# Layer 0's first phase and layer 1's stick-breaking heads in another order

## Chip, core and metric

The kernel runs on one core of one Trainium2 chip. The time is the device time of one execution in microseconds. Three runs of the kernel before gave 1487.02, 1489.60 and 1493.04 us.

## What is computed

A two-layer causal decoder trunk for one sequence of 512 tokens, 1024 wide, in float32. Both touched stages start from the adaLN modulation and end in a projection:

```python
c_act = jax.nn.silu(c)
mod = c_act @ ada_w[layer] + ada_b[layer]
sh_m, sc_m, g_m, sh_f, sc_f, g_f = [t[:, None, :] for t in jnp.split(mod, 6, axis=-1)]
hm = x * (1.0 + sc_m) + sh_m
...
z = jnp.einsum('bqhd,bkhd->bhqk', q_blk, k) * scale
causal = s_pos[None, :] < t_pos[:, None]
log_1m = jnp.where(causal, jax.nn.log_sigmoid(-z), 0.0)
suffix = lax.cumsum(log_1m, axis=3, reverse=True)
excl = jnp.pad(suffix[..., 1:], ((0, 0), (0, 0), (0, 0), (0, 1)))
att = jnp.where(causal, jnp.exp(jax.nn.log_sigmoid(z) + excl), 0.0)
return jnp.einsum('bhqk,bkhd->bqhd', att, v)
...
y = jnp.concatenate([oc, od], axis=-1) @ w_out
```

The first four lines open both touched mixers; the next are one block of 128 queries of the eight stick-breaking heads of layer 1, whose output `oc` is joined with `od` of the dilated attention (three groups of four heads, merged by their softmax denominators). Layer 0 projects `hm` for gated linear attention and mLSTM.

## The kernel before

Every large product is made of three matmuls: the float32 operands are split into a high part (`w_hi`, `h_hi`) and a rest (`w_lo`, `h_lo`), and hi x lo, hi x hi and lo x hi are added in PSUM. Weights come as a stream of slots of 128x1024. SP loads slot s into one of four `raw` buffers, ACT makes `w_hi` (`to_hi`, L690), POOL makes `w_lo` (L670), and TensorE uses both from a ring of four. ACT's order is written by hand: `hi_until(n)` makes all splits up to slot n, and `ahead(name)` those for a stage and three more. TensorE waits for a slot in `slot_waits`, and reports it used with `slot_done`.

**First phase.** The shift and scale of layer 0 are needed in quarters: quarter p covers chunks 2p and 2p+1 of the 1024 features. For each quarter DVE multiplies eight blocks of `ada_first` by the columns of `c_act` and adds them up in `ada_acc` (`first_block`, 128x512 each, L1631 and L1634). TensorE then sums over the partitions, four matmuls against a column of ones (`first_cols`, L1175), DVE adds the bias (`first_mod`, L1641, L1643), ACT scales the input chunk into `tmp` (`x_scaled`, L719) and makes `h_hi` (L704), DVE makes `h_lo` (L1570). TensorE then does the 18 matmuls of chunk k, 12 for `va` and 6 for `qa` (`first_va`, `first_qa`). All four quarters run one after another; the narrow projection follows.

**Layer 1.** After the panels of q, k and v of the stick-breaking heads, each head h goes through: `sb_z` (TensorE, scores into 1280 columns of PSUM), Abs, Exp, Ln (ACT, `sb_first`), softplus and two masks (DVE, `softplus`, L2025, L2027), `sb_tri` (TensorE adds the suffix sums to the same PSUM columns), Exp (ACT, `sb_second`), two masks (DVE, `att_mask`), `sb_av` (TensorE). Between them stand the fillers, the list `FILL`: six panels of 48 matmuls (two slots each) for q and k of the dilated heads, and the two groups `vd0` (four slots) and `vd1` (two slots) of their values. With filler i stands either tri (i even) or av and the next z (i odd), so that the eight fillers lie in heads 0 to 3; heads 4 to 7 follow without. Here z of one head can be issued ahead, since odd heads above 4 use other PSUM columns (`sb_col`). Each pair of heads fills one chunk of the input of the output projection: DVE copies it to `tmp` and ACT and DVE split it (`sb_chunk`). Then come 16 score steps of the dilated heads (TensorE, L1497), each read by DVE (L2077, with maxima L2082), the turned maxima, and the transposes and products of the dilated heads (`turn_round`, `pv_round`), and `out1`.

## Time and profile before

| | |
|---|---|
| median of three runs | 1489.6 us |
| the profiled execution | 1487.6 us |
| its span, first to last instruction | 1485.8 us |
| mean granted TensorE clock | 0.959 |
| TensorE matmul, busy | 1366.9 us (92%) |
| TensorE weight load | 1123.3 us (76%) |
| DVE | 622.7 us (42%) |
| ACT | 449.3 us (30%) |
| POOL | 506.8 us (34%) |

The span is 1.8 us shorter than the time of that execution. Times in the trace are counted from the span's start. A busy TensorE is not one at its peak, since the ends of matmuls are modelled; consecutive matmuls overlap in the rows.

### The profile page before, as it was taken

Reading aid. Unit: us, or ns where it says so; the run is one execution under the profiler, and the core shown is the slowest. Engines: PE = TensorE matmul, PEld = TensorE weight load, DVE = VectorE, ACT = ScalarE, POOL = GpSimd, SP = SyncE. Lnnn points to the kernel's source line nnn. Section 1 sums busy time; section 2 is a strip of 40 time slices with the busy share of each in tenths; the row PEclk is TensorE's granted clock in tenths of the full one; section 3 lists DMA queues with packets and bytes.
Section 4 is the critical chain, followed back from the end, with each engine's and each line's share of the span. In section 5 each row is a group of like instructions: output and inputs, shape, how many; then the busy total and the mean of one; then the engine's idle time right before and its main releaser. Section 6 shows DMA issues by size and latency. Waiting matters only on the chain.

```text
span 1485.8 us, 17068 instructions
## 1 busy us (share of the span) xinstructions
PE 1366.9 (92%) x6510; PEld 1123.3 (76%) x6510; DVE 622.7 (42%) x830; ACT 449.3 (30%) x603; POOL 506.8 (34%) x209
## 2 busy tenths in 40 slices
PE   3799998798999999999899999887889999999995
PEld 3678776588888888888788778656779888887884
DVE  5569751858643433400882232226486111010007
ACT  2343233314233223212323323333233323322121
POOL 2334331024345344444243333100125444444440
PEclk9899998799999999999999999997999999999998
DMA  9493632042556546643235322001113232234311
GB/s 335 134 97 102 212 117 82 22 176 72 181 175 209 197 152 232 182 126 100 104 116 180 109 85 72 29 1 57 36 50 100 99 99 99 92 79 154 99 57 56
DMA packets 93456, 173.79 MB, mean 117 GB/s; under 512 B 15655, under 2 KB 61879, under 8 KB 93276
## 3 DMA queue, kind: packets, MB, share of 16 engines
q1 hardware_dynamic: 90264, 169.63, 36.8%
q10 hardware_dynamic: 3140, 3.43, 0.9%
q8 instruction: 38, 0.62, 0.2%
q14 instruction: 14, 0.11, 0.0%
HBM read 170.87 MB, written 4.52 MB: 118 GB/s over the span
## 4 chain that ended last, share of the span: by engine, by line
PE 64%; issue 22%; DVE 6%; POOL 6%; ACT 2%; POOLq 0%; DVEq 0%; ACTq 0%
PE ps L1018 12%; PE ps L1020 12%; PE ps L1019 12%; PE ps L1050 6%; PE ps L1051 6%; PE ps L1052 6%; POOL w_lo L670 6%; PE ps L1462 1%; PE ps L1143 1%; PE ps L1145 1%; PE ps L1144 1%; PE ps L1434 1%; PE ps L1445 1%; PE ps L1448 1%; DVE rec L2101 1%
## 5 line engine op out<-in xcount | busy, mean ns | idle before, releaser
L670 POOL TENSOR_TENSOR w_lo<-raw,w_hi 128x1024 fp32r<-128x1024 f32 x205 | 506.6, 2474 | 943.8 <-ACT w_hi L690 943.4
L1018 PE MATMUL ps<-h_lo,w_hi 128*128 128x512 f32 (+2 forms) x1064 | 401.6, 377 | 13.6 <-DVE tmp L1867 6.2
L1019 PE MATMUL ps<-h_hi,w_hi 128*128 128x512 f32 (+2 forms) x1064 | 398.0, 374 | 0.0
L1020 PE MATMUL ps<-h_hi,w_lo 128*128 128x512 f32 (+2 forms) x1064 | 397.4, 374 | 0.0
L690 ACT ACTIVATE w_hi<-raw 128x1024 fp32r<-128x1024 f32 x205 | 216.0, 1056 | 487.8 <-PE ps L1052 189.0
L1018 PEld LDWEIGHTS ps<-h_lo,w_hi 128*128 128x128 f32 (+1 forms) x1064 | 204.1, 192 | 54.4 <-DVE tmp L1867 7.5
L1020 PEld LDWEIGHTS ps<-h_hi,w_lo 128*128 128x128 f32 (+1 forms) x1064 | 203.9, 192 | 35.1
L1019 PEld LDWEIGHTS ps<-h_hi,w_hi 128*128 128x128 f32 (+1 forms) x1064 | 203.9, 192 | 34.0
L1951 DVE TENSOR_TENSOR tmp<-tmp,ps 128x512 f32<-128x512 f32 x44 | 30.1, 688 | 264.2 <-PE ps L1020 264.2
L1050 PE MATMUL ps<-w_hi,hid_lo 128*128 128x512 f32 x352 | 137.9, 392 | 1.8 <-issue 0.9
L1052 PE MATMUL ps<-w_lo,hid_hi 128*128 128x512 f32 x352 | 137.5, 390 | 0.0
L1051 PE MATMUL ps<-w_hi,hid_hi 128*128 128x512 f32 x352 | 137.4, 390 | 0.0
L1901 DVE TENSOR_TENSOR ps<-ps,gate_ffn 128x1024 f32<-128x1024 f32 x8 | 9.8, 1229 | 184.5 <-PE ps L1052 184.5
L1050 PEld LDWEIGHTS ps<-w_hi,hid_lo 128*128 128x128 f32 x352 | 66.5, 189 | 16.1 <-issue 1.3
L1586 DVE SCALAR_TENSOR_TENSOR ada_acc<-ada_raw,c_act,ada_acc 128x1024 f32<-128x1024 f32 x35 | 63.4, 1813 | 35.3 <-DMA ada_raw<-astream 34.3
L1051 PEld LDWEIGHTS ps<-w_hi,hid_hi 128*128 128x128 f32 x352 | 66.5, 189 | 13.7
L1052 PEld LDWEIGHTS ps<-w_lo,hid_hi 128*128 128x128 f32 x352 | 66.4, 189 | 13.8
L1970 DVE SCALAR_TENSOR_TENSOR ada_acc<-ada_raw,c_act,ada_acc 128x1024 f32<-128x1024 f32 x35 | 54.8, 1565 | 46.5 <-DMA ada_raw<-astream 46.1
L1143 PE MATMUL ps<-w_hi,h_lo 128*128 128x512 f32 (+1 forms) x192 | 74.1, 386 | 0.0
L1144 PE MATMUL ps<-w_hi,h_hi 128*128 128x512 f32 (+1 forms) x192 | 72.8, 379 | 0.0
L1145 PE MATMUL ps<-w_lo,h_hi 128*128 128x512 f32 (+1 forms) x192 | 72.7, 379 | 0.0
L908 ACT ACTIVATE hid_hi<-tmp 128x512 f32 (+1 forms) x44 | 27.5, 631 | 88.5 <-DVE tmp L1951 88.5
(228 smaller groups left out, 1491.5 us busy)
## 6 DMA issues: line engine op xcount, KB each, us to landing
raw<-wstream SPq DMA_DIRECT2D x205, 512.0 KB, 4.1
ada_raw<-astream SPq DMA_DIRECT2D x80, 512.0 KB, 4.6
ada_first<-astream SPq DMA_DIRECT2D x12, 512.0 KB, 10.0
ln_rows<-row_scratch SPq DMA_DIRECT2D x3, 1024.0 KB, 6.8
skew_scratch<-f_scratch ACTq DMA_DIRECT2D x1, 2304.0 KB
ada_first<-astream SPq DMA_DIRECT2D x8, 256.0 KB, 4.6
xa<-xT SPq DMA_DIRECT2D x4, 512.0 KB, 9.4
out<-xa SPq DMA_DIRECT2D x4, 512.0 KB, 3.5
```

Of the source, the lines that this page charges most:

```text
L670: nc.gpsimd.tensor_tensor(w_lo[:, slot, :], raw[:, slot % RAW, :], w_hi[:, slot, :].bitcast(F32), ALU.subtract).then_inc(sem("w_lo_ready"), 1)
L690: nc.scalar.activation(w_hi[:, slot, :], raw[:, slot, :], ACT.Copy).then_inc(sem("w_hi_ready"), 1)
L1018: pe.matmul(o, w_h, x_l, start=start, stop=False)
L1019: pe.matmul(o, w_h, x_h, start=False, stop=False)
L1020: return pe.matmul(o, w_l, x_h, start=False, stop=stop)
L1050: pe.matmul(o, x_lo, w_h, start=k == 0, stop=False)
L1051: pe.matmul(o, x_hi, w_h, start=False, stop=False)
L1052: m = pe.matmul(o, x_hi, w_l, start=False, stop=k == nk - 1)
L1143: pe.matmul(o, h_lo[:, k, tokens], w_hi[:, s % RING, w], start=start, stop=False)
L1144: pe.matmul(o, h_hi[:, k, tokens], w_hi[:, s % RING, w], start=False, stop=False)
L1145: m = pe.matmul(o, h_hi[:, k, tokens], w_lo[:, s % RING, w], start=False, stop=stop)
L1586: V.scalar_tensor_tensor(ada_acc[:], src, c_act[:, k:k + 1], ada_acc[:], ALU.mult, ALU.add).then_inc(sem("ada_step"), 1)
```

## The change

In the first phase the first slot of weights is loaded behind the first pair of `ada_first` and split before anything else on ACT. DVE adds up only six of eight blocks per quarter (`ON_DVE`); the products of blocks 6 and 7 are made by TensorE, added in PSUM to the column sums, so that `first_cols` has twelve matmuls in place of four. The column sums of quarter p+1 are issued between the two chunks of quarter p, and DVE's steps for the next quarter stand between the two `h_lo` of this one.

In layer 1 the fillers alternate q and k panels, with `vd1` before `vd0`, and one filler stands with each of the eight heads. All heads use the same PSUM columns and one bank for av; z(h+1) waits for the Exp of head h (`att_exp`). `vd0` has two slots with head 7, the third before av(7) and the fourth behind score step 3. The score steps use banks 4 to 7. The finished chunks are staged (`staged`) in `ada_acc` and `tmp`, and split only after the heads: the hi on ACT behind the copies of `vd0`, the lo on DVE behind `nm`.

```diff
@@ -91,14 +91,20 @@
+ON_DVE = 6
...
+FILL = ("qd0", "kd0", "qd1", "kd1", "qd2", "kd2", "vd1", "vd0")
+MIXED = [n for n in STAGES if n not in FILL]
+MIXED[MIXED.index("out10"):MIXED.index("out10")] = FILL
 def slot_table():
...
-    for name in STAGES:
+    for name in MIXED:
@@ -407,15 +410,12 @@
-    AV_BANK = (7, 7, 7, 3)
-    def sb_col(h):
-        return 0 if h > 4 and h % 2 else 4 * S
-    FILL = [f"qd{p}" for p in range(3)] + [f"kd{p}" for p in range(3)] + ["vd0", "vd1"]
+    AV_BANK = 7
+    SB_COL = 4 * S
+    def staged(n):
+        return ada_acc[:, n * S:(n + 1) * S] if n < 2 else tmp[:, n % 2, :]
@@ -448,7 +448,7 @@
     def score_bank(s):
...
-        return (0, 1, 2, 4)[2 * (part % 2) + h % 2]
+        return 4 + 2 * (part % 2) + h % 2
     def part_tiles(part):
@@ -571,10 +571,11 @@
-        for k in range(0, KC, 2):
+        load_pair(0, 0, 2)
+        load(0)
+        for k in range(2, KC, 2):
...
-        load(0)
@@ -719,12 +720,13 @@
+        hi_until(1)
         for p in range(4):
             for n in (2 * p, 2 * p + 1):
...
-                if p == 0:
-                    hi_until(n + 1)
+                if n == 0:
+                    hi_until(2)
...
         def x_chunk(n):
@@ -955,32 +957,31 @@
         def sb_second(h):
...
-            nc.scalar.activation(sb_a[h % 2][:], psf[:, sb_col(h):sb_col(h) + SC], ACT.Exp).then_inc(sem("att_exp"), 1)
+            nc.scalar.activation(sb_a[h % 2][:], psf[:, SB_COL:SB_COL + SC], ACT.Exp).then_inc(sem("att_exp"), 1)
...
-        for i, part in enumerate(FILL):
-            if part[0] == "v":
+        for h, part in enumerate(FILL):
+            if part == "vd0":
+                hi_until(SLOTS[part][0] + 2 + RING)
+            elif part[0] == "v":
...
-            if i == 1:
+            if h == 1:
...
-            if i % 2 == 0:
-                sb_second(i // 2)
-            else:
-                sb_first(i // 2 + 1)
-        hi_of_chunk(H_BASE["cat1"], 0)
-        for h in range(4, 8):
+            sb_second(h)
...
-            sb_second(h)
-            if h % 2 == 0:
-                hi_of_chunk(H_BASE["cat1"] + h // 2 - 1, h // 2 - 1)
-        hi_of_chunk(H_BASE["cat1"] + 3, 3)
+        hi_until(SLOTS["vd0"][0] + 4 + 2)
+        v_blocks("vd0", v_dst["vd0"])
+        for n in range(4):
+            e = H_BASE["cat1"] + n
+            act.wait_ge(sem("h_tmp_ready"), e + 1)
+            nc.scalar.activation(h_hi[:, n, :], staged(n), ACT.Copy).then_inc(sem("h_hi_ready"), 1)
         def dil_exp(h, kind):
@@ -1123,11 +1124,12 @@
-        def group(name, kk_n, width, beside=None):
+        def group(name, kk_n, width, beside=None, only=None):
...
-            wait_pair(pe, name)
-            for i in range(count):
+            if only is None or 0 in only:
+                wait_pair(pe, name)
+            for i in range(count) if only is None else only:
@@ -1168,11 +1170,17 @@
         def first_cols(p):
-            pe.wait_ge(sem("first_step"), KC * (p + 1))
+            pe.wait_ge(sem("c_ready"), 1)
+            pe.wait_ge(sem("first_step"), ON_DVE * (p + 1))
+            if p == 0:
+                pe.wait_ge(sem("in_ada0_6"), 32)
             for blk in range(2):
...
-                    m = pe.matmul(ps[:, 6 + p % 2, 2 * blk + c:2 * blk + c + 1], ada_acc[:, a:a + P], ones[:], start=True, stop=True)
+                    o = ps[:, 6 + p % 2, 2 * blk + c:2 * blk + c + 1]
+                    pe.matmul(o, ada_acc[:, a:a + P], ones[:], start=True, stop=False)
+                    for k in range(ON_DVE, KC):
+                        m = pe.matmul(o, ada_first[:, p, k, blk, tile_of(c)], c_act[:, k:k + 1], start=False, stop=k == KC - 1)
...
         def first_va(k):
@@ -1200,16 +1208,18 @@
+        first_cols(0)
         for p in range(4):
-            first_cols(p)
             for k in (2 * p, 2 * p + 1):
...
-                    if k in (0, 2, 4, 6):
+                    if k % 2 == 0 and part is first_va:
...
-                    if k in (0, 4):
+                    if k in (0, 4) and part is first_qa:
...
+                if k % 2 == 0 and p < 3:
+                    first_cols(p + 1)
@@ -1423,13 +1433,11 @@
         def sb_z(h):
...
-            base = sb_col(h)
+            base = SB_COL
...
-            elif h <= 4:
+            else:
...
-            elif h >= 6:
-                pe.wait_ge(sem("att_exp"), h - 1)
@@ -1454,50 +1462,51 @@
-            if h == 2:
-                pe.wait_ge(sem("staged"), 1)
-            if h == 4:
-                pe.wait_ge(sem("h_tmp_ready"), H_BASE["cat1"] + 2)
+            if h in (2, 4, 6):
+                pe.wait_ge(sem("h_tmp_ready"), H_BASE["cat1"] + h // 2)
...
-                m = pe.matmul(ps[r:r + 64, AV_BANK[c], j * P:S], vc[:, j, h * 64:h * 64 + 64], sb_a[h % 2][:, OFS[j]:OFS[j] + WID[j]],
+                m = pe.matmul(ps[r:r + 64, AV_BANK, j * P:S], vc[:, j, h * 64:h * 64 + 64], sb_a[h % 2][:, OFS[j]:OFS[j] + WID[j]],
...
-        for i, part in enumerate(FILL):
-            if part[0] == "v":
-                group(part, 2 if part == "vd0" else 4, S if part == "vd0" else 256)
+        for h, part in enumerate(FILL):
+            if part == "vd0":
+                group(part, 2, S, only=(0, 1))
+            elif part == "vd1":
+                group(part, 4, 256)
...
-            if i % 2 == 0:
-                sb_tri(i // 2)
-            elif i < 7:
-                sb_av(i // 2)
-                sb_z(i // 2 + 1)
-        sb_z(4)
-        wait_free(pe, "vd1")
-        wait_free(pe, "vd1+")
-        for h in range(4, 8):
+            sb_tri(h)
+            if h:
+                sb_av(h - 1)
...
-            sb_av(h - 1)
-            sb_tri(h)
+        group("vd0", 2, S, only=(2,))
...
-        pe.wait_ge(sem("att_exp"), 8)
-        for s in range(16):
+        def scores(s):
...
+            if score_bank(s) == AV_BANK:
+                pe.wait_ge(sem("h_tmp_ready"), H_BASE["cat1"] + 4)
...
+        for s in range(4):
+            scores(s)
+        group("vd0", 2, S, only=(3,))
+        for s in range(4, 16):
+            scores(s)
@@ -1538,7 +1547,8 @@
-        pe.wait_ge(sem("h_tmp_ready"), H_BASE["cat1"] + 4)
+        wait_free(pe, "vd0")
+        wait_free(pe, "vd0+")
@@ -1618,19 +1628,18 @@
-        def first_block(p):
+        def first_block(p, ks):
...
-            if p >= 2:
-                dve.wait_ge(sem("first_cols"), p - 1)
-            for k in range(KC):
-                step = KC * p + k
+            for k in ks:
...
+                    if p >= 2:
+                        dve.wait_ge(sem("first_cols"), p - 1)
...
-                    dve.wait_ge(sem("first_step"), step)
+                    dve.wait_ge(sem("first_step"), ON_DVE * p + k)
@@ -1642,11 +1651,21 @@
-        for p in range(4):
-            first_block(p)
+        first_block(0, range(ON_DVE))
+        first_mod(0)
+        lo_of_chunk(H_BASE["in"], 0)
+        lo_of_chunk(H_BASE["in"] + 1, 1)
+        first_block(1, range(ON_DVE))
+        for p in range(1, 4):
...
-            for n in (2 * p, 2 * p + 1):
-                lo_of_chunk(H_BASE["in"] + n, n)
+            if p < 3:
+                first_block(p + 1, range(0, 2))
+            lo_of_chunk(H_BASE["in"] + 2 * p, 2 * p)
+            if p < 3:
+                first_block(p + 1, range(2, 4))
+            lo_of_chunk(H_BASE["in"] + 2 * p + 1, 2 * p + 1)
+            if p < 3:
+                first_block(p + 1, range(4, ON_DVE))
...
         def v_blocks(name):
@@ -2033,38 +2052,28 @@
-        def sb_chunk(n):
-            e = H_BASE["cat1"] + n
+        def stage(n):
...
-            tmp_free(e)
-            src = ada_acc[:, 0:S] if n == 0 else ps[:, AV_BANK[n], :]
-            V.tensor_copy(tmp[:, e % 2, :], src).then_inc(sem("h_tmp_ready"), 1)
-            lo_of_chunk(e, n)
+            V.tensor_copy(staged(n), ps[:, AV_BANK, :]).then_inc(sem("h_tmp_ready"), 1)
+        def lo_of_staged(n):
+            dve.wait_ge(sem("h_hi_ready"), H_BASE["cat1"] + n + 1)
+            V.tensor_tensor(h_lo[:, n, :], staged(n), h_hi[:, n, :].bitcast(F32), ALU.subtract).then_inc(sem("h_ready"), 1)
...
-        for i, part in enumerate(FILL):
-            if part[0] == "v":
+        for h, part in enumerate(FILL):
+            if part == "vd1":
...
-            else:
+            elif part != "vd0":
...
-            if i % 2 == 0:
-                att_mask(i // 2)
-            else:
-                if i == 3:
-                    dve.wait_ge(sem("av_done"), 2)
-                    V.tensor_copy(ada_acc[:, 0:S], ps[:, AV_BANK[0], :]).then_inc(sem("staged"), 1)
-                softplus(i // 2 + 1)
-        dve.wait_ge(sem("staged"), 1)
-        sb_chunk(0)
-        for h in range(4, 8):
+            att_mask(h)
+            if h in (2, 4, 6):
+                stage(h // 2 - 1)
...
-            att_mask(h)
-            if h % 2 == 0:
-                sb_chunk(h // 2 - 1)
-        sb_chunk(3)
+        stage(3)
@@ -2081,6 +2090,7 @@
+        v_blocks("vd0")
@@ -2088,6 +2098,8 @@
+        for n in range(4):
+            lo_of_staged(n)
         def dil_out(h):
```

ACT at the start of the program, before:

```order
L711 ACTIVATE c_act<-vec 128x8
L719 ACTIVATE tmp<-xa,mod,scl 128x512
L704 ACTIVATE h_hi<-tmp 128x512
L690 ACTIVATE w_hi<-raw 128x1024
L719 ACTIVATE tmp<-xa,mod,scl 128x512
L704 ACTIVATE h_hi<-tmp 128x512
L690 ACTIVATE w_hi<-raw 128x1024 x2
L719 ACTIVATE tmp<-xa,mod,scl 128x512
```

and now:

```order
L712 ACTIVATE c_act<-vec 128x8
L691 ACTIVATE w_hi<-raw 128x1024
L720 ACTIVATE tmp<-xa,mod,scl 128x512
L705 ACTIVATE h_hi<-tmp 128x512
L691 ACTIVATE w_hi<-raw 128x1024
L720 ACTIVATE tmp<-xa,mod,scl 128x512
L705 ACTIVATE h_hi<-tmp 128x512
L691 ACTIVATE w_hi<-raw 128x1024
```

The first split of a weight has moved ahead of the first scaled chunk, the second stands between the first two chunks.

DVE in the first phase, from the first accumulation of quarter 1 on, before:

```order
L1631 TENSOR_SCALAR ada_acc<-ada_first,c_act 128x512
L1634 SCALAR_TENSOR_TENSOR ada_acc<-ada_first,c_act,ada_acc 128x512 x7
L1641 TENSOR_TENSOR mod<-ps,vec 128x2x2
L1643 TENSOR_SCALAR scl<-mod 128x2
L1570 TENSOR_TENSOR h_lo<-tmp,h_hi 128x512 x2
L1631 TENSOR_SCALAR ada_acc<-ada_first,c_act 128x512
L1634 SCALAR_TENSOR_TENSOR ada_acc<-ada_first,c_act,ada_acc 128x512 x7
```

and now:

```order
L1640 TENSOR_SCALAR ada_acc<-ada_first,c_act 128x512
L1643 SCALAR_TENSOR_TENSOR ada_acc<-ada_first,c_act,ada_acc 128x512 x5
L1650 TENSOR_TENSOR mod<-ps,vec 128x2x2
L1652 TENSOR_SCALAR scl<-mod 128x2
L1640 TENSOR_SCALAR ada_acc<-ada_first,c_act 128x512
L1643 SCALAR_TENSOR_TENSOR ada_acc<-ada_first,c_act,ada_acc 128x512
L1580 TENSOR_TENSOR h_lo<-tmp,h_hi 128x512
L1643 SCALAR_TENSOR_TENSOR ada_acc<-ada_first,c_act,ada_acc 128x512 x2
L1580 TENSOR_TENSOR h_lo<-tmp,h_hi 128x512
L1643 SCALAR_TENSOR_TENSOR ada_acc<-ada_first,c_act,ada_acc 128x512 x2
L1650 TENSOR_TENSOR mod<-ps,vec 128x2x2
```

A quarter has six accumulations in place of eight; those of quarter 2 now stand around the two `h_lo` of quarter 1.

TensorE in layer 1, from the last matmul of tri(5) to the first of tri(6), before (L1434 is z, L1462 is av, L1445 is tri):

```order
L1445 MATMUL ps<-sb_sp_113,cst 128x128
L1434 MATMUL ps<-qc,kc 128x512
L1434 MATMUL ps<-qc,kc 128x384
L1434 MATMUL ps<-qc,kc 128x256
L1434 MATMUL ps<-qc,kc 128x128
L1462 MATMUL ps<-sb_a_111,vc 64x512
L1462 MATMUL ps<-sb_a_111,vc 64x384
L1462 MATMUL ps<-sb_a_111,vc 64x256
L1462 MATMUL ps<-sb_a_111,vc 64x128
L1445 MATMUL ps<-sb_sp_112,cst 128x512
```

and now, from the last matmul of a tri to the first of the panel behind the next z (L1453 is tri, L1468 is av, L1442 is z, L1019 to L1021 are a panel's):

```order
L1453 MATMUL ps<-sb_sp_112,cst 128x128
L1468 MATMUL ps<-sb_a_111,vc 64x512
L1468 MATMUL ps<-sb_a_111,vc 64x384
L1468 MATMUL ps<-sb_a_111,vc 64x256
L1468 MATMUL ps<-sb_a_111,vc 64x128
L1442 MATMUL ps<-qc,kc 128x512
L1442 MATMUL ps<-qc,kc 128x384
L1442 MATMUL ps<-qc,kc 128x256
L1442 MATMUL ps<-qc,kc 128x128
L1019 MATMUL ps<-h_lo,w_hi 128x512
L1020 MATMUL ps<-h_hi,w_hi 128x512
L1021 MATMUL ps<-h_hi,w_lo 128x512
```

Where tri(6) followed av(5) directly, a filler of 48 matmuls now stands behind z.

## Rows read from the trace of the kernel before

**Rows 1.** The page, part 1: busy time of each engine, share of the span, instructions.
```profile
PE 1366.9 (92%) x6510; PEld 1123.3 (76%) x6510; DVE 622.7 (42%) x830; ACT 449.3 (30%) x603; POOL 506.8 (34%) x209
```

**Rows 2.** Windows, first phase: stretch, length, busy us per engine (count), clock, DMA.
```profile
0.00:22.90 22.90, 1.89 (x9) 1.83 (x9) 10.80 (x15) 6.16 (x8) 5.30 (x6) 1.00 0.94 317
...
66.70:76.50 9.80, 9.80 (x36) 7.97 (x37) 1.42 (x3) 3.52 (x5) 4.73 (x2) 0.83 0.71 55
```

**Rows 3.** Timeline, DVE, first phase: start, us, engine, line, operation, tiles, count.
```profile
9.60 3.18 DVE L1634 SCALAR_TENSOR_TENSOR ada_acc<-ada_first,c_act,ada_acc 128x512 f32<-128x512 f32 x4 [0.87 <-DMA ada_first<-astream]
...
14.74 0.16 DVE L1641 TENSOR_TENSOR mod<-ps,vec 128x4 f32<-128x4 f32 x1 [1.96 <-PE ps L1175]
...
16.64 0.69 DVE L1570 TENSOR_TENSOR h_lo<-tmp,h_hi 128x512 fp32r<-128x512 f32 x1 [1.54 <-ACT h_hi L704]
...
23.06 7.47 DVE L1634 SCALAR_TENSOR_TENSOR ada_acc<-ada_first,c_act,ada_acc 128x512 f32<-128x512 f32 x7
...
39.43 9.63 DVE L1634 SCALAR_TENSOR_TENSOR ada_acc<-ada_first,c_act,ada_acc 128x512 f32<-128x512 f32 x7
```

**Rows 4.** Timeline, TensorE, first phase.
```profile
12.83 1.87 PE L1175 MATMUL ps<-ones,ada_acc 128*128 128x1 f32 x8 [12.83 <-DVE ada_acc L1634]
...
22.88 0.77 PE L1185 MATMUL ps<-w_hi,h_lo 128*128 128x512 f32 x1 [8.18 <-POOL w_lo L670]
...
49.11 1.49 PE L1175 MATMUL ps<-ones,ada_acc 128*128 128x1 f32 x8 [2.97 <-DVE ada_acc L1634]
53.29 0.80 PE L1185 MATMUL ps<-w_hi,h_lo 128*128 128x512 f32 x1 [2.69 <-DVE h_lo L1570]
...
63.04 0.95 PE L1175 MATMUL ps<-ones,ada_acc 128*128 128x1 f32 x8
```

**Rows 5.** Timeline, ACT, first phase: the first half of a weight split.
```profile
16.52 1.04 ACT L690 ACTIVATE w_hi<-raw 128x1024 fp32r<-128x1024 f32 x1
```

**Rows 6.** Windows, layer 1, head 0 to the start of out1.
```profile
813.50:947.10 133.60, 133.60 (x608) 109.35 (x608) 32.35 (x30) 43.86 (x44) 43.57 (x18) 0.98 0.28 87
947.10:998.90 51.80, 42.14 (x154) 24.34 (x153) 15.87 (x27) 21.80 (x19) 0.00 (x0) 0.93 0.00 0
998.90:1020.30 21.40, 13.59 (x121) 12.72 (x120) 20.37 (x27) 0.63 (x1) 0.00 (x0) 0.81 0.16 41
1020.30:1057.60 37.30, 27.08 (x201) 25.19 (x201) 23.57 (x20) 17.98 (x42) 0.00 (x0) 0.82 0.08 33
```

**Rows 7.** Timeline, head 1 of layer 1, all engines, in order of time.
```profile
846.44 1.24 ACT L950 ACTIVATE sb_a<-ps 128x1280 f32<-128x1280 f32 x1 [6.77 <-PE ps L1434]
...
851.32 4.95 POOL L670 TENSOR_TENSOR w_lo<-raw,w_hi 128x1024 fp32r<-128x1024 f32 x2 [11.37 <-ACT w_hi L690]
851.85 4.70 DVE L2027 TENSOR_TENSOR sb_sp<-sb_sp,cst 128x256 f32<-128x256 f32 x2
...
857.39 1.02 PE L1445 MATMUL ps<-sb_sp,cst 128*128 128x512 f32 x2
...
861.92 1.24 ACT L958 ACTIVATE sb_a<-ps 128x1280 f32<-128x1280 f32 x1 [6.46 <-PE ps L1445]
...
872.73 2.37 PE L1462 MATMUL ps<-sb_a,vc 128*64 128x512 f32 x8
```

**Rows 8.** Timeline, heads 4 to 6 of layer 1, DVE and TensorE.
```profile
954.99 0.76 DVE L2027 TENSOR_TENSOR sb_sp<-sb_sp,cst 128x256 f32<-128x256 f32 x2
955.81 1.13 PE L1445 MATMUL ps<-sb_sp,cst 128*128 128x512 f32 x2 [2.34 <-DVE sb_sp L2027]
...
961.74 2.42 PE L1434 MATMUL ps<-qc,kc 64*128 64x512 f32 x8 [1.33 <-ACT sb_a L958]
```

**Rows 9.** Waits, 813 to 1058 us: waited for, us in total, times, longest.
```profile
PE ps L1462 <- DVE sb_a L2033: 4.6, 2, 2.5
```

**Rows 10.** Timeline, DVE, score steps and first turn copy.
```profile
1006.40 2.21 DVE L2077 TENSOR_TENSOR lg_loc<-ps,bt 128x512 f32<-128x512 f32 x4
...
1028.82 0.69 DVE L2109 COPY pt<-ps 128x512 f32<-128x512 f32 x1 [3.86 <-PE ps L1522]
```

More of the change, by code:

```diff
@@ L333, in last @@
         return first + n - 1
-    V_FREE = {"va": 0, "vb": 1, "vc": 2, "vd0": 3, "vd1": 4}
+    V_FREE = {"va": 0, "vb": 1, "vc": 2, "vd1": 3, "vd0": 4}
     def group(name, free0, free1):
@@ L357, in build_program @@
             if layer == 1:
-                for i, (name, panels) in enumerate((("qc", 2), ("kc", 2), ("qd", 3), ("kd", 3))):
-                    base = (0, 2, 4, 7)[i]
-                    for p in range(panels):
-                        e = base + p
-                        use(f"{name}{p}", [("qk1_act", e + 1), ("qk1_dve", e + 1)], last(f"{name}{p}"))
-                    if name == "kc":
+                for e, name in enumerate(("qc0", "qc1", "kc0", "kc1") + FILL[:6]):
+                    use(name, [("qk1_act", e + 1), ("qk1_dve", e + 1)], last(name))
+                    if name == "kc1":
                         vgroup("vc")
+                vgroup("vd1")
                 vgroup("vd0")
-                vgroup("vd1")
         else:
@@ L944, in sb_first @@
         def sb_first(h):
-            z = psf[:, sb_col(h):sb_col(h) + SC]
+            z = psf[:, SB_COL:SB_COL + SC]
             a = sb_a[h % 2]
@@ L1438, in sb_tri @@
         def sb_tri(h):
-            base = sb_col(h)
+            base = SB_COL
             sp_ = sb_sp[h % 2]
@@ L2024, in softplus @@
             sp_ = sb_sp[h % 2]
-            link(V.scalar_tensor_tensor(sp_[:], psf[:, sb_col(h):sb_col(h) + SC], 0.0, sb_a[h % 2][:], ALU.max, ALU.add))
+            link(V.scalar_tensor_tensor(sp_[:], psf[:, SB_COL:SB_COL + SC], 0.0, sb_a[h % 2][:], ALU.max, ALU.add))
             for t in diag_tiles(sp_):
```

## The prediction

> **What bounds the kernel now.** The page says that TensorE is busy 1366.9 of 1485.8 us, a share of 92% [rows 1]. The other engines only matter where TensorE waits for them, so I read its waits stage by stage. The windows give two stages that the diff touches. The first phase, to the start of the narrow projection at 76.5 us: no real matmul runs before 22.9 us, and from 66.7 to 76.5 us the granted clock is 0.83 of full [rows 2]. The stick-breaking stage of layer 1: from 813.5 to 947.1 us TensorE has no idle time (133.60 of 133.60), from 947.1 to 998.9 it is busy 42.14 of 51.80, from 998.9 to 1020.3 busy 13.59 of 21.40 while DVE is busy 20.37 [rows 6]. So in the last window DVE sets the pace; in the one before it the heads 4 to 7 do, one after another, with nothing to fill their waits.
>
> The timelines say what those waits are. First phase: the column sums of a quarter wait for DVE's last accumulation (49.11, idle 2.97), and the first chunk behind them waits 2.69 us for the chain mod, scale, x_scaled, hi, lo (53.29) [rows 4]; that matmul takes 0.80 us, at the slow level of the clock (1.2 GHz), and the next six are as slow. Layer 1: tri(4) waits 2.34 us, z(6) 1.33 and z(7) the same again [rows 8], av(6) and av(7) 4.6 us together [rows 9]: 9.6 us in all.
>
> **Layer 1, part by part.** One filler now goes with each of the eight heads, where eight fillers went with heads 0 to 3. The fillers' work is the same, save that the last slot of vd0 moves behind four score steps. Its price is one quarter of vd0, 24 matmuls. A panel has 48: tri(1) and the panel behind it take 872.73 - 857.39 = 15.3 us [rows 7], tri(4) alone 961.74 - 1.33 - 955.81 = 4.6 [rows 8] with some 0.2 of overlap, so the panel is 10.9 us and a matmul 0.227. The slot is 24 x 0.227 = 5.5 us.
>
> - Full-clock work in 947.1 to 998.9: tri 4 x 4.5, av 5 x 2.3, z 4 x 2.4 [rows 7, 8] = 39.1 us. The window lasts 51.8: 9.6 idle and 3.0 slow clock are over it.
> - With a filler behind every z the same work is issued in 133.6 + 39.1 us less the moved slot, 5.5, plus one new wait: z(1) follows tri(0) with no av between them and waits for the Exp, 1.3 us. From head 1 on, av(h-1), 2.3 us, stands where this 1.33 us wait was, and hides it. av(7) ends at 813.5 + 133.6 + 39.1 - 5.5 + 1.3 = 982.0, so 16.9 us earlier.
> - Is the softplus in time for each tri? Abs, Exp and Ln start at 846.44 behind z(1); DVE's masks end at 851.85 + 4.70 = 856.55; tri(1) starts at 857.39 [rows 7]. That is the situation in which every head now is: 0.8 us to spare. If the cover were gone, each head would wait.
> - ACT carries per head 4 x 1.25 for the head [rows 7] and 2 x 1.05 for splits [rows 5], with a panel copy under 8 of some 20 us; its Exp is queued behind two weight splits, which have long been done when tri ends [rows 7]. POOL does two splits of 2.5 us per head. The four hi and four lo of the staged chunks go behind the heads: ACT has nothing to do there until nm is ready, and DVE waits 3.86 us before its first turn copy [rows 10], against 4 x 0.69 = 2.8 for the lo. The stage copies (0.69) stand while ACT works on z. Hidden, all of it. vd0's two DVE copies, 1.4 us, lie in the transposes that DVE waits for. If that cover goes, 1.4 us come back.
> - The bias loads, the row order of weights and SP's queue keep their order relative to the slots; no transfer is added.
> - Score steps: DVE needs stage, memset and steps 0 to 3 with their maxima, some 0.7 + 0.5 + 4.8 = 6.0 us behind av(7). TensorE does four steps (2.8; sixteen took 13.59 at clock 0.81 [rows 6], 0.7 each at the full one), the slot (5.5) and step 4 (0.7) = 9.0. DVE so waits 3.0 us, then does the rest, 1006.40 to 1020.3 = 13.9 [rows 6, 10]: 22.9 against 21.4 now (where a hi and a lo stood in the way). **1.5 us are given back.** Layer 1: -16.9 + 1.5 = **-15.4 us**. Bounds: -19 if DVE were never held up and the stretch at the end kept the full clock, -7 if each head waited 1 us.
>
> **First phase, part by part.**
> - Raw 0 is loaded and split first. Its POOL split (some 2.5 us, half of 4.95 [rows 7]) now stands beside the first accumulations. DVE steps cost 0.80 us (3.18 for four) [rows 3]. Two drop out, -1.6; the 0.5 MB that now go ahead and POOL's presence take about as much. I take 0; bounds -1.6 and +2.5, one POOL split.
> - Column sums have 24 records in place of 8. They took 1.87 us for the first quarter, 1.49 at the half clock, 0.95 at the full one [rows 4]: three times as much less the fixed part is 5.3 at the slow level and 2.8 at the fast one. So +3.4 for the first, then 3 x 1.9.
> - The first chunk no longer waits for w_lo. It started at 22.88 after a wait for POOL [rows 4], though h_lo was done at 17.33 [rows 3]. Now mod is at 12.8 + 5.3 = 18.2, and h_lo, as much behind it as before (17.33 - 14.74 = 2.6), at 20.8. The chunk starts **2 us** earlier.
> - Column sums of quarter p+1 stand between the two chunks of quarter p. The 2.69 waits (three) disappear under them. But DVE has to be in time. Quarter 1: hi(1) is done at 18.2 + 1.9 + a split of 1.04 [rows 5] + 1.4 = 22.5, lo(1) comes behind POOL's split of slot 1 and ends at 24.3. Six steps take 4.3 us of their own and lose 2.2 to one split (7.47 for seven steps where 5.3 is their own time [rows 3]): 30.8. TensorE does the first chunk, 14 matmuls at 0.43 and 4 at 0.23, by 28.0 and waits 2.8; sums to 33.6. Quarter 2: DVE's mod, two steps, lo, two steps, lo take to 38.4, the last two steps 1.5 and 4.4 lost to two splits (9.63 for seven [rows 3]), some 0.5 of it over before: 43.8, TensorE 33.6 + 8.2 = 41.8, it waits 2.0; sums to 46.6. Quarter 3: DVE 51.4 + 1.5 + 2.2 = 55.1, TensorE 54.8; sums to 57.9, three more chunks of 4.1.
> - The last chunk ends at 70.2 against 76.5 in this reckoning at the full clock, -6.3. But a wait of 2 to 3 us followed by column sums is what stood before the slow matmuls at 53.29 and 66.7 (clock 0.83, [rows 2, 4]): 7 or 8 matmuls at 0.43 in place of 0.23 are 1.5 us each time. Twice, with half absorbed where DVE is late anyway: +1.8. First phase: **-4.5 us**. Bounds: -11, if DVE is in time and the clock stays up; +2, if all waits stay and both slow stretches too.
>
> At one place a rule can be weighed. The two masks of 128x256 took 4.70 us beside 4.95 us of POOL splits and 0.76 alone [rows 7, 8], a loss of 3.94. The Trainium skill, page "SBUF — State Buffer", section "Who interferes with whom", says that DVE and GpSimd share one port pair as an exclusive lock and the one that comes second is held up entirely. By that rule taken to its end the masks lose the whole 4.95, 1.0 us more, which is 0.2 beyond the slack; the sum would be 8 x 0.2 = 1.6 us worse. The sum goes by the measured row.
>
> **The sum.** -15.4 - 4.5 = -19.9. The profiled execution took 1487.6 us outside (span 1485.8 and 1.8 around it): 1487.6 - 19.9 = 1467.7, so **1468 us**. That execution stood 2.0 us below the median of the runs, 1489.6.
>
> **The rivals.** About 0.5% (7.4 us) is what a measurement can tell; the line for faster is 1482 us.
> 1. The first phase gives nothing: longer column sums and DVE's lateness eat the earlier start. For it: both chains I computed leave 2 to 3 us waits. Then 1487.6 - 15.4 = 1472.
> 2. The masks come late at every head, by 1.5 us: two splits fall on each softplus, and the slack is 0.8 us. 8 x 1.5 = 12, so 1480. Against it: just this overlap is there now, in time [rows 7].
> 3. More than the forecast: DVE in time in the first phase, clock full in both places, 1487.6 - 28 = 1460.
> 4. **Slower.** z(h+1) uses the same PSUM columns as head h and now waits at each head for its Exp, so all heads form one loop: z 2.4, Abs to Ln 3.9, DVE 6.3, tri 4.5, Exp 1.3 = 18.4 us, against 20.2 us of TensorE work per head (panel 10.9, tri, av, z). ACT's Exp is queued behind weight splits: where a weight lands late, the Exp is late. The loop decides from 20.2 us on; the gain is gone at 23 us, and it is slower by 0.5% from 24.1. At 26 us: 7 x 5.8 = 41, 1508. Against it: TensorE was never idle in 813.5 to 947.1 [rows 6], so no weight was late.
> 5. The diff does not fill the heads (order of slots and fillers out of step): no change, 1488. The order of instructions shows panels behind z(5) to z(7), so next to nothing.
>
> **How the numbers follow.** Forecast 0.62 (1460 to 1475), rival 1 0.15, rival 2 0.10, rival 3 0.10, rival 4 0.02, rival 5 0.01. The range 1459 to 1478 holds the forecast, rivals 1 and 3 and the edge of rival 2; 0.15 lies outside. Faster: 0.62 + 0.15 + 0.10 and half of rival 2, 0.92. Same: the other half, rival 5 and a little for tails, 0.06. Slower 0.02.
>
> **What would show it.** Right: no idle time on TensorE from tri(1) to av(7) and av(7) near 978 on the new time axis (982 less 4.5); z(1) waiting 1.3; DVE waiting some 3 us before score step 4; the first 128x512 matmul near 21 us and the narrow projection near 72; column sums of 24 records at 2.8 us or more. Wrong: waits before each tri (rival 2), before each z (rival 4), or a narrow projection at 76 or later (rival 1).

## The result, and the profile after

| | median us | lowest to highest | runs |
|---|---|---|---|
| before | 1491.14 | 1487.02 to 1493.04 | 4 |
| changed | 1472.15 | 1469.38 to 1474.12 | 4 |

The ratio is 0.9891, with a 95% interval from 0.987 to 0.9912: 1.1% faster, inside the range of 1459 to 1478, 4 us above the forecast of 1468, and just where rival 1 stood (1472). That ratio, which is not the quotient of the two medians, stands for 16 us; the medians are 19.0 us apart. The profiled execution took 1471.77 us (span 1470.0), against 1487.59 (span 1485.8) before: 15.8 us less, where the sum said 19.9. Of the runs of the kernel before that stand beside experiments 5 to 8 one took 4254.8 us; the ratios leave it out.

**Layer 1.** Windows of the changed kernel from z(1) to the start of out1; the columns are those of [rows 6].

```profile
832.30:982.30 150.00, 149.98 (x669) 114.38 (x669) 55.85 (x47) 54.09 (x50) 36.94 (x15) 1.00 0.19 60
982.30:1006.10 23.80, 16.96 (x145) 16.11 (x144) 19.80 (x27) 3.27 (x6) 0.00 (x0) 0.85 0.14 54
1006.10:1042.30 36.20, 25.94 (x201) 24.05 (x201) 27.15 (x26) 18.01 (x42) 0.00 (x0) 0.83 0.02 10
```

From z(1) to av(7) TensorE is never idle. Its waits from 815 to 985 us, over all lines, are one row:

```profile
PE ps L1442 <- ACT sb_a L960: 1.3, 1, 1.3
```

That is the wait of z(1) for the Exp that the forecast named. The rest is told by these rows of the changed kernel's timelines: POOL and DVE in head 2, TensorE at tri(2), and DVE at the score steps.

```profile
859.74 4.93 POOL L671 TENSOR_TENSOR w_lo<-raw,w_hi 128x1024 fp32r<-128x1024 f32 x2 [15.14 <-ACT w_hi L691]
860.28 4.68 DVE L2046 TENSOR_TENSOR sb_sp<-sb_sp,cst 128x256 f32<-128x256 f32 x2
865.77 1.02 PE L1453 MATMUL ps<-sb_sp,cst 128*128 128x512 f32 x2
...
979.98 2.37 PE L1468 MATMUL ps<-sb_a,vc 128*64 128x512 f32 x8
982.38 0.69 DVE L2058 COPY tmp<-ps 128x512 f32<-128x512 f32 x1 [8.50 <-PE ps L1468]
992.21 2.22 DVE L2086 TENSOR_TENSOR lg_loc<-ps,bt 128x512 f32<-128x512 f32 x4 [3.44 <-PE ps L1500]
1006.14 1.86 PE L1515 MATMUL ps<-cst,cols 128*4 128x128 f32 x8 [5.24 <-DVE cols L2091]
```

The masks end at 864.96, tri(2) starts at 865.77: the 0.8 us of slack, the same in heads 1 to 5; heads 6 and 7 have 1.3 to 1.4. av(7) is done at 982.3, where the forecast said 982.0 before it took off the 4.5 us of the first phase. DVE then waits 3.44 us for score step 4 (forecast 3.0).

**First phase.** Timeline of TensorE in the changed kernel. Column sums are now printed by pairs of rows, x2 on L1181 (ones) and x4 on L1183 (the two products), four pairs per quarter; the first row of each quarter's sums and the first of the chunk behind them:

```profile
14.29 0.56 PE L1181 MATMUL ps<-ones,ada_acc 128*128 128x1 f32 x2 [14.29 <-DVE ada_acc L1643]
...
22.23 0.80 PE L1193 MATMUL ps<-w_hi,h_lo 128*128 128x512 f32 x1 [2.69 <-DVE h_lo L1580]
...
32.09 0.35 PE L1181 MATMUL ps<-ones,ada_acc 128*128 128x1 f32 x2 [3.67 <-DVE ada_acc L1643]
...
36.41 0.77 PE L1193 MATMUL ps<-w_hi,h_lo 128*128 128x512 f32 x1
...
47.00 0.35 PE L1181 MATMUL ps<-ones,ada_acc 128*128 128x1 f32 x2 [0.57 <-DVE ada_acc L1643]
...
59.58 0.28 PE L1181 MATMUL ps<-ones,ada_acc 128*128 128x1 f32 x2
```

And DVE's: the last four accumulations of quarter 0, the first and the last mod (the shift and scale of a quarter, with the bias added), and two of the places where POOL's splits hold it.

```profile
9.23 4.95 DVE L1643 SCALAR_TENSOR_TENSOR ada_acc<-ada_first,c_act,ada_acc 128x512 f32<-128x512 f32 x4 [2.33 <-DMA ada_first<-astream]
19.58 0.16 DVE L1650 TENSOR_TENSOR mod<-ps,vec 128x4 f32<-128x4 f32 x1 [5.39 <-PE ps L1183]
...
25.34 2.61 DVE L1640 TENSOR_SCALAR ada_acc<-ada_first,c_act 128x512 f32<-128x512 f32 x1
...
41.16 5.69 DVE L1643 SCALAR_TENSOR_TENSOR ada_acc<-ada_first,c_act,ada_acc 128x512 f32<-128x512 f32 x2
...
62.35 0.16 DVE L1650 TENSOR_TENSOR mod<-ps,vec 128x4 f32<-128x4 f32 x1 [4.25 <-PE ps L1183]
```

DVE ends quarter 0 at 14.18 though it does two steps fewer; it ended at 12.78 before [rows 3]. The first sums take from 14.29 to 19.5, the first chunk starts at 22.23 (22.88 before [rows 4]), and every later mod comes later than the forecast had it. The narrow projection starts at 76.15, against 76.52 before: in this trace the first phase gives 0.4 us of the 4.5 forecast, which is what rival 1 said.

TensorE's waits up to 76 us say where the gain went, first of the kernel before, then of the changed one (us in total, times, longest):

```profile
PE ps L1175 <- DVE ada_acc L1634: 15.8, 2, 12.8
PE ps L1185 <- POOL w_lo L670: 8.2, 1, 8.2
PE ps L1185 <- DVE h_lo L1570: 8.1, 3, 2.7
```

```profile
PE ps L1181 <- DVE ada_acc L1643: 18.5, 3, 14.3
PE ps L1193 <- DVE h_lo L1580: 2.7, 1, 2.7
```

The waits fell from 32.1 to 21.2 us, 10.9 less. The four sets of column sums took 5.25 us before and take 14.8 now, 9.6 more, and the 144 matmuls of the chunks took 39.2 and take 40.1, 0.9 more. The order did remove waits; the longer sums used them up.

### The profile page after: what moved, and what is told of

Its sections match the earlier page's. It is cut to its first block, busy times and chain, and to the rows that moved or that the text cites. A ratio compares the mean times of both kernels' runs of the same rounds, so it can differ in the third digit from the quotient of the medians.

```text
span 1470.0 us, 17183 instructions
## 1 busy us (share of the span) xinstructions
PE 1371.6 (93%) x6574; PEld 1131.7 (77%) x6574; DVE 636.7 (43%) x821; ACT 449.1 (31%) x603; POOL 513.7 (35%) x209
## 4 chain that ended last, share of the span: by engine, by line
PE 80%; DVE 10%; issue 6%; ACT 1%; POOL 1%; DMA 0%; DVEq 0%; POOLq 0%; ACTq 0%
PE ps L1019 14%; PE ps L1020 14%; PE ps L1021 14%; PE ps L1051 7%; PE ps L1052 7%; PE ps L1053 7%; PE ps L1145 2%; PE ps L1147 2%; PE ps L1146 2%; PE ps L1442 1%; POOL w_lo L671 1%; PE ps L1468 1%; PE ps L1456 1%; PE ps L1453 1%; PE ps L1158 1%
## 5 line engine op out<-in xcount | busy, mean ns | idle before, releaser
L671 POOL TENSOR_TENSOR w_lo<-raw,w_hi 128x1024 fp32r<-128x1024 f32 x205 | 513.5, 2509 | 921.1 <-ACT w_hi L691 920.6
L1019 PE MATMUL ps<-h_lo,w_hi 128*128 128x512 f32 (+2 forms) x1064 | 403.2, 379 | 13.1 <-DVE tmp L1886 6.2
L1021 PE MATMUL ps<-h_hi,w_lo 128*128 128x512 f32 (+2 forms) x1064 | 398.7, 375 | 0.0
L1019 PEld LDWEIGHTS ps<-h_lo,w_hi 128*128 128x128 f32 (+1 forms) x1064 | 204.9, 193 | 53.4 <-DVE tmp L1886 7.5
L1021 PEld LDWEIGHTS ps<-h_hi,w_lo 128*128 128x128 f32 (+1 forms) x1064 | 204.9, 193 | 35.1
L1053 PEld LDWEIGHTS ps<-w_lo,hid_hi 128*128 128x128 f32 x352 | 66.1, 188 | 13.9
```

The costliest lines, as they stand in the source:

```text
L671: nc.gpsimd.tensor_tensor(w_lo[:, slot, :], raw[:, slot % RAW, :], w_hi[:, slot, :].bitcast(F32), ALU.subtract).then_inc(sem("w_lo_ready"), 1)
L1019: pe.matmul(o, w_h, x_l, start=start, stop=False)
L1021: return pe.matmul(o, w_l, x_h, start=False, stop=stop)
L1053: m = pe.matmul(o, x_hi, w_l, start=False, stop=k == nk - 1)
```

## The experiments

Theory A: layer 1 gives what the sum said, and the first phase next to nothing, because (i) the two products of each quarter cost TensorE more than the two steps cost DVE, and (ii) w 0 ahead of the weights of quarter 0 makes DVE late, by its transfer and by POOL's split. Rival B: the first phase did gain its 4.5 us, and another stage lost them. The mark for the first phase is the start of va's first eviction on ACT (74.30 in the changed kernel, 74.67 before). Each median stands beside before's on the same chip: 1487.57 for 1 to 4, 1487.23 for 5 to 8, 1486.94 for the rest.

**1 and 2. Each half of the change alone.** e1 has the first phase of before: `for p in range(4): first_block(p); first_mod(p)`, then the two lo, `first_cols(p)` ahead of both chunks, eight accumulations per quarter, and w 0 (the first slot of weights) at its old place. e2 has before's layer 1.

> The first phase of the kernel before, layer 1 of the changed one. Theory A (layer 1 gives all the gain, the first phase 0.4 us, read at va's first copy: 74.30 in the changed kernel, 74.67 before): about 1472.5 us, ratio to before 0.990, va's first copy at 74.7, av(7) starting at 980.4, the first turn of the first output at 1013. Rival B (the first phase does give its 4.5 us and later stages lose them again): about 1476, and somewhere behind 75 us a stretch that is shorter here than in the changed kernel.

> The first phase of the changed kernel, layer 1 of the one before. Theory A: within 1 us of before, ratio 0.9995, va's first copy at 74.3. Rival B: 4.5 us less than before, ratio 0.997.

e1: 1472.47, ratio 0.9901 (0.988 to 0.9922). av(7) starts 167.8 us behind the Abs of head 0, 166.6 in the changed kernel, 181.3 before (994.87 less 813.53): layer 1 gives its gain by itself. e2: 1484.35, ratio 0.9975 (0.9963 to 0.9988), though va's first copy is at 74.3 in its trace. The trace speaks for A, the median for something between: 3.2 us less, not 1. The profiled execution of e2 was the slowest of its twelve (1488.23), that of e1 lay 5.1 us above the median (1477.55). The disagreement came back in 11 and 12.

**3. No products on TensorE.**

```diff
-ON_DVE = 6
+ON_DVE = 8
-    pe.matmul(o, ada_acc[:, a:a + P], ones[:], start=True, stop=False)
+    m = pe.matmul(o, ada_acc[:, a:a + P], ones[:], start=True, stop=ON_DVE == KC)
```

> The changed kernel with all eight accumulations of each quarter on DVE and none on TensorE; the next quarter's column sums still stand between the chunks, w 0 is still split ahead. Theory A1 (the two accumulations on TensorE, 16 records more per quarter at one column each, cost more than the two DVE steps that they replace: 3.4 us for the first quarter and 1.9 to 3 for the others, against 1.6 us of two DVE steps): the first sums start at 15.8 and end at 17.7 in place of 19.5, the first chunk starts at 20.4 in place of 22.23, and each later mod is 1 to 3 us earlier; the first phase ends 3 to 5 us earlier than in the changed kernel, va's first copy near 70, the time near 1468. Rival A2 (DVE bounds the first phase, whatever TensorE's sums cost): each of the quarters 1 to 3 ends on DVE 1.6 us or more later, va's first copy at 75 to 79 and the time 1473 to 1477.

1467.28, ratio 0.9866 (0.9847 to 0.9886). Timeline of TensorE in e3:

```profile
15.58 1.84 PE L1179 MATMUL ps<-ones,ada_acc 128*128 128x1 f32 x8 [15.58 <-DVE ada_acc L1641]
20.12 0.80 PE L1191 MATMUL ps<-w_hi,h_lo 128*128 128x512 f32 x1 [2.69 <-DVE h_lo L1578]
...
31.42 1.84 PE L1179 MATMUL ps<-ones,ada_acc 128*128 128x1 f32 x8 [5.01 <-DVE ada_acc L1641]
...
45.28 1.02 PE L1179 MATMUL ps<-ones,ada_acc 128*128 128x1 f32 x8 [1.47 <-DVE ada_acc L1641]
```

va's first copy is at 69.31, 5.0 us earlier, as A1 had it. The first sums start 1.3 us later and end 2.1 us earlier. TensorE waits longer for quarter 1 (5.01 against 3.67) and still gains: over the first phase its waits are 26.4 us, 5.2 more than in the changed kernel, and its sums 5.7 us, 9.1 less. What counts is when the sums end, and a product record costs as much as a record of ones. The first copy lies 3.6 us below the earliest of five executions with the changed first phase (72.87). The medians agree in direction, but the interval of this ratio, like that of 4, overlaps the changed kernel's.

**4. w 0 loaded at its old place.**

```diff
-load_pair(0, 0, 2)
-load(0)
-for k in range(2, KC, 2):
+for k in range(0, KC, 2):
     load_pair(0, k, 2)
 load_x(0)
+load(0)
```

> The changed kernel with w 0 loaded behind all weights of quarter 0 again (ACT still splits it before it waits for the first mod). Theory: 0.5 MB ahead of the second pair of adaLN weights and the POOL split beside DVE's steps are why DVE ends its first quarter at 14.2 and not at 12.7. Then it ends at 12.7 here, the first column sums start there and end at 18.0, the first chunk starts at 20.7 in place of 22.23 (w 0 is split by 20.2, from its landing at 16.5 in the kernel before), and va's first copy comes up to 1.5 us earlier, about 73: 1471. Rival: DVE's steps are late for another reason (its own rate with six steps), they end at 14 again, and w 0 split late holds the first chunk at 22.5 or later: no gain or a loss of 1 us.

1466.61, ratio 0.9856 (0.9836 to 0.9876); va's first copy at 70.09. Timeline of e4, DVE then TensorE:

```profile
7.73 3.18 DVE L1642 SCALAR_TENSOR_TENSOR ada_acc<-ada_first,c_act,ada_acc 128x512 f32<-128x512 f32 x4 [0.95 <-DMA ada_first<-astream]
...
11.01 0.56 PE L1180 MATMUL ps<-ones,ada_acc 128*128 128x1 f32 x2 [11.01 <-DVE ada_acc L1642]
...
19.02 0.80 PE L1192 MATMUL ps<-w_hi,h_lo 128*128 128x512 f32 x1 [2.76 <-DVE h_lo L1579]
```

The four steps start 1.5 us earlier (7.73 for 9.23) and take 3.18 us in place of 4.95. So w 0 ahead costs 3.3 us, 1.5 before DVE's four steps can start and 1.8 beside POOL's split, more than I expected here: six steps end at 10.9, and 12.7 was the end of eight. (In the six traces that have w 0 ahead and six steps, the first sums start at 13.9 to 15.0.) w 0 is split by 16.7 all the same, before the first chunk needs it.

**5. Both undone** (the edits of 3 and 4).

> Both undone at once: all eight accumulations on DVE, w 0 loaded behind the weights of quarter 0. If the two costs lie in a row, mod of quarter 0 is at 14.7 (17.5 and 16.3 with one undone, 19.6 with none), the first chunk starts at 17.3, the mods of quarters 1 to 3 come at 30.5, 43.7 and 54.6, va's first copy at 66.5 against 69.3 and 70.1, the time near 1464.5. Rival: the transfers bound the first phase (the DMA queues are full to 45 us), so the steps of quarters 1 and 2 wait for their weights, and va's first copy stays at 68 or later: 1467.

1465.32, ratio 0.9847 (0.9823 to 0.9871), va's first copy at 68.68. The gain is 5.6 us, less than the two in a row (9.2). No step of a later quarter waits for its weights, so it is not their transfers. Timeline of e5, POOL and DVE:

```profile
14.91 2.34 POOL L670 TENSOR_TENSOR w_lo<-raw,w_hi 128x1024 fp32r<-128x1024 f32 x1 [14.46 <-ACT w_hi L690]
15.35 1.92 DVE L1649 TENSOR_SCALAR scl<-mod 128x2 f32<-128x2 f32 x1
```

The split of w 0 now starts just ahead of the scale column, an instruction of 0.17 us that takes 1.92: it ends with the split, at 17.3. That does not explain all of it, though: e9 and e10 below keep these two edits and have the same delay, yet their mod is at 14.1 and 14.6 (15.15 here) and va's first copy at 65.24 and 65.33, where the two gains in a row would put it. Beside e9, e5 lost 1.0 us because the second pair of its first weights landed later (DVE's six steps start at 8.31, not 7.29), 0.8 us in the sums of quarter 1, which ran at the slow level (1.84 for 1.02), and 1.6 us in a slow stretch behind the sums of quarter 3 that e9 does not have. The code of the first phase is the same in both, so one profiled execution tells a position in it only to some 3 us.

**6. Sums behind both chunks.**

```diff
-if k % 2 == 0 and p < 3:
+if k % 2 and p < 3:
     first_cols(p + 1)
```

> The changed kernel with the column sums of quarter p+1 behind the second chunk of quarter p, not between the two. Theory (moving them between the chunks is the one part of the first phase that gains): TensorE does chunk 1 while DVE finishes quarter 1 and has no wait there, 3.7 us less, but it waits 2.7 us for mod, x, hi and lo behind each of three sums, 8.1 us more, and the chunk behind each wait begins at the slow level: va's first copy near 77 against 74.3, the time 1475. Rival (between the chunks TensorE waits for DVE as long as it would wait for the chain): va's first copy within 1 us of 74.3.

1472.92, ratio 0.9906 (0.9887 to 0.9924). Waits of TensorE in e6, to 76 us:

```profile
PE ps L1181 <- DVE ada_acc L1643: 14.3, 1, 14.3
PE ps L1193 <- DVE h_lo L1580: 10.8, 4, 2.7
```

In the changed kernel these rows are 18.5 (3 times) and 2.7 (once). As expected, the waits for the accumulations are gone and three more of 2.7 us are there. va's first copy is at 78.71, 4.4 us later, behind all five executions of the changed first phase. So in the trace the place between the chunks is the part that gains. The runs show less: the profiled execution, 1481.58, was the slowest of seven, and the ratio, 0.9906, lies within the interval of the changed kernel's 0.9891.

**7. vd0's last slot in four blocks** (`only=(3,), tbs=(s // 2 - 2,)` ahead of steps 4, 6, 8, 10).

> The changed kernel with vd0's last slot cut into its four token blocks of six matmuls, ahead of score steps 4, 6, 8 and 10, in place of all 24 ahead of step 4. Theory: DVE's 3.4 us wait for score step 4 goes, and since DVE sets the end of the score steps, the maxima are done 3.4 us earlier and so is all behind them: 1468.7, the transposes of the maxima at 1002.7. Rival (DVE's wait was cover for something else, an eviction or a load that comes next): the wait appears in another step and the transposes stay at 1005 to 1006.

1469.67, ratio 0.9888 (0.9867 to 0.9909). The rival's case: DVE's wait went to two other steps, 3.08 us in all (timeline of e7).

```profile
991.14 1.02 DVE L2088 TENSOR_TENSOR lg_loc<-ps,bt 128x384 f32<-128x384 f32 x2 [1.15 <-PE ps L1501]
...
997.66 1.29 DVE L2088 TENSOR_TENSOR lg_dil<-ps,bt 128x512 f32<-128x512 f32 x2 [1.93 <-PE ps L1501]
```

TensorE had no gap from 980 to 998: the blocks stood too early, not too close together. The ratio is that of the changed kernel (0.9891) within the noise.

**8. The masks three times over**, in each head's softplus.

```diff
-for t in diag_tiles(sp_):
-    i = V.tensor_tensor(t, t, twice(keep), ALU.mult)
+for n in range(3):
+    for t in diag_tiles(sp_):
+        i = V.tensor_tensor(t, t, twice(keep), ALU.mult)
+    if n < 2:
+        link(i)
```

> The changed kernel with each head's two masks multiplied in three times over (the result is the same): four more DVE instructions per head behind the ones that POOL holds up, 0.38 us each alone and some 0.05 between them, 1.7 us in all. Theory (DVE ends its masks 0.8 us before tri starts, in heads 1 to 7 alike): TensorE waits 0.9 us before tri in each of seven heads, tri(1) starts at 846.6, av(7) 6 us later than 979.98, the time 1478. Rival 2 of the prediction had its price right but its slack wrong: with no real slack it would be 7 x 1.7 = 12, 1484; with a slack of over 1.7 us, no change.

1476.18, ratio 0.992 (0.9901 to 0.994). Timeline of e8, tri(1) and tri(2) on TensorE, DVE between them:

```profile
844.59 1.13 PE L1453 MATMUL ps<-sb_sp,cst 128*128 128x512 f32 x2 [0.68 <-DVE sb_sp L2047]
859.28 6.28 DVE L2047 TENSOR_TENSOR sb_sp<-sb_sp,cst 128x256 f32<-128x256 f32 x6
865.62 1.13 PE L1453 MATMUL ps<-sb_sp,cst 128*128 128x512 f32 x2 [0.67 <-DVE sb_sp L2047]
```

1.6 us more on DVE give a wait of 0.7, and these two tri stand 21.03 us apart in place of 20.09: 0.94 more per head, of which the wait itself is 0.7. Six heads waited, 3.5 us in all. av(7) starts 172.4 us behind the Abs of head 0 in place of 166.6, 5.8 us later; 6 were expected. The slack of 0.8 us is real: what goes beyond it costs time at nearly every head, which is rival 2's mechanism, and the change stays just short of it.

**9. All three**, with the slot's blocks ahead of steps 6, 8, 10 and 12.

> Three edits together on the changed kernel: all accumulations of the first phase on DVE, w 0 loaded at its old place, and vd0's last slot in four blocks of six matmuls ahead of score steps 6, 8, 10 and 12 (ahead of 4, 6, 8 and 10 it left waits of 1.15 and 1.93 us, because TensorE was busy from 982 to 998 without a gap). If DVE's wait at the first steps was TensorE's work standing too early, the waits fall from 3.4 us in all to about 0.8, the transposes come 2.6 us nearer to av(7) (23.5 us behind its start, 26.1 in the changed kernel), and the time is 1465.3 - 2.6 = 1462.7. If TensorE is the bound there whatever the order, they stay at 25.9 and the time at 1465.

**1463.11, ratio 0.9834 (0.9813 to 0.9854): faster than both kernels, and with e10 the best.** Its interval lies below both of the changed kernel's (the table above and 11); it overlaps that of e5, so the runs alone do not tell what the slot's new place adds. Timeline of e9:

```profile
989.64 1.29 DVE L2085 TENSOR_TENSOR lg_dil<-ps,bt 128x512 f32<-128x512 f32 x2 [1.14 <-PE ps L1498]
...
997.87 1.87 PE L1514 MATMUL ps<-cst,cols 128*4 128x128 f32 x8 [3.67 <-DVE cols L2090]
```

The transposes start 23.6 us behind the start of av(7), 26.2 in the changed kernel. 1.2 of these 2.55 us are lost again before out1: 37.35 us lie between the two, 36.13 in the changed kernel. The matmuls behind the transposes are slow in both, and here 12 more of them are, at 0.21 us in place of 0.11. (The kernel before had nearly the same: 37.28 us.) TensorE's idle time ahead of the transposes is 3.67 us here and 5.24 there; that this is the cause was not tried.

**10. And two steps of quarter 1 ahead of lo(1).**

```diff
 lo_of_chunk(H_BASE["in"], 0)
+first_block(1, range(0, 2))
 lo_of_chunk(H_BASE["in"] + 1, 1)
-first_block(1, range(ON_DVE))
+first_block(1, range(2, ON_DVE))
```

> The same with the first two accumulations of quarter 1 put on DVE between the lo of chunk 0 and the lo of chunk 1, where DVE waits 1.6 us for ACT (quarters 2 and 3 have this order in the changed kernel). If their weights have landed by 19.5 us, quarter 1's sums come 1.2 us earlier (mod at 31.4 in place of 32.6) and va's first copy at 67.5: 1461.5. If POOL's split, which starts at 19.8, holds them as it held lo of chunk 1, or their weights land later, the gain is under 0.3 us or lo of chunk 1 is late: 1463.

1463.12, ratio 0.9848 (0.9827 to 0.9868); mod of quarter 1 at 30.89, 30.82 in e9. No gain, by POOL (timeline of e10): the step that takes 0.75 us takes 2.79.

```profile
19.47 2.79 DVE L1642 SCALAR_TENSOR_TENSOR ada_acc<-ada_first,c_act,ada_acc 128x512 f32<-128x512 f32 x1
```

**11 and 12. The changed kernel and e1 again, on one chip.**

> The changed kernel again, beside the next one on the same chip: what its first phase is worth in the medians. By the profile (va's first copy 73.4 to 74.3 in four executions with this first phase, 74.5 and 74.7 in two with the old one) it should be 0.7 us less than the next one; by the run with the changed first phase alone, whose median was 3.2 us under before, 3 us less. About 1472.

> The first phase of before with layer 1 of the changed kernel, again: 1472.5 to 1475, and va's first copy at 74.6.

1470.15, ratio 0.9878 (0.9857 to 0.9899), and 1474.0, ratio 0.9917 (0.9899 to 0.9934): 3.9 us apart. The timelines of ACT, e11 then e12:

```profile
72.87 0.60 ACT L742 ACTIVATE va<-ps 128x512 f32<-128x512 f32 x1 [6.57 <-PE ps L1195]
```

```profile
72.63 0.60 ACT L739 ACTIVATE va<-ps 128x512 f32<-128x512 f32 x1 [4.00 <-PE ps L1186]
```

Over all traces va's first copy is at 72.87 to 74.30 with the new first phase (five executions), at 72.63 to 74.67 with the old one (three). So these medians give the first phase 3.9 us and those of e2 3.2; the ratios of the changed kernel and e1 (0.9891 and 0.9901) differ by only 1.5 us; and the profiled executions give nothing that stands out of their spread. That of e12 was the fastest of its six, 5 us below the median. **This stays open.** Behind va's copy the code is the same up to head 0 of layer 1, yet that stretch took 737.7 to 741.2 us with the new first phase and 737.7 to 742.5 with the old one: it varies by as much as is looked for, and one profiled execution per kernel can't place it. Most of the variation is in TensorE's own busy time: the same 3408 matmuls were busy for 702.7 us in e8 and 706.8 in e2, both with the new first phase, and the waits came to 35.0 and 34.3.

## Why the prediction was right, and where it was wrong

- **The heads (forecast -16.9): right.** av(7) ended at 982.3 for 998.9 before, -16.6. z(1) waited 1.3 us, nothing waited before any tri. e8 shows that the slack was what the row said.
- **Score steps (+1.5): too small.** DVE's wait was 3.44 for 3.0, and from the end of av(7) to the transposes it took 23.8 us, not 22.9: 21.4 before, so 2.4 were given back. The moved slot took 6.0 us, not 5.5, from 985.02 to 991.02. 1.15 us came back by out1 (36.13 us behind the transposes, 37.28 before). Layer 1 as a whole: out1 starts at 1042.27 for 1057.60, -15.3, forecast -15.4. Two errors of about 1 us that cancel: that this sum came out to 0.1 us is luck.
- **First phase (-4.5): wrong in the trace.** The step that failed first is "Two drop out, -1.6; the 0.5 MB that now go ahead and POOL's presence take about as much. I take 0". They took 3.3 (e4: sums at 11.01, not 14.29), which leaves the sums 1.46 us later than before. It lay inside the bound of +2.5, and the row for the upper end was there: a POOL split holds DVE for its own length.
- The length of the first sums was right (5.25 us for 5.3), and so was that of two others (2.8 and 2.7). Those of quarter 1 took 4.3: behind the wait of 3.67 us the slow level came in the midst of them. With the later start their end is at 36.4 for 33.6, and the ends of quarters 2 and 3 at 49.8 and 62.3 for 46.6 and 57.9.
- The clock cost more than the forecast gave it. It had two slow stretches and 1.8 us for both. Slow matmuls of 128x512 followed the sums of all three later quarters: 8 or 9 each time, 0.2 us each, 5.4 us together, and 1.1 of them came back in the first chunk, which took 6.0 us, not 7.1. The third stretch begins at 63.66, behind sums before which TensorE had not waited. Added up over the phase, 4.1 us were missing: about 0.7 in waits, 1.1 in the sums and 2.4 in the chunks' matmuls.
- What the forecast did not ask was whether the products are worth their place at all. It had their price, +3.4 and 3 x 1.9, and what it set against that was two DVE steps of 0.8 us per quarter. e3 shows the balance: 5.0 us in the traces, on a position that scatters by 1.4 us in five executions of the changed first phase.
- **The total.** -19.9 forecast, -15.8 between the two profiled executions, -16 by the ratio, -19.0 between the medians. The medians are nearest to the forecast, but since the trace does not show the first phase's share, that is no proof of its steps.
- **Rivals.** 1 is what the trace of the first phase shows, in its number and in its reason (longer sums and DVE's lateness eat the earlier start). 2 was near (0.8 us). 4, the loop through the same PSUM columns, did not decide: 20.09 us per head, as TensorE's work made it, against 20.2 reckoned.

## What to carry to other kernels

A step moved from a vector engine to TensorE is priced by what TensorE's records cost at the level of the clock it will have there, on the chain that waits for them: here two DVE steps, 1.6 us, were changed for 16 records, 3.4 us at the slow level and 1.8 at the full one. When a load is moved ahead, count the engine that splits it: its split stands beside whatever the vector engine then does. Here an engine's wait went away when the work that caused it was moved to where the other engine waits (e9); cutting that work finer in nearly the same place only spread the wait over two steps (e7).
